# Five statistics of a two-block transformer layer as two rounded products each

## The chip, the cores and the metric

One core of one Trainium2 chip runs the kernel. The metric is the time of one execution on the device in microseconds; a time is the median over runs, and profiles are of one execution. TensorE is called PE, VectorE DVE, ScalarE ACT, GpSimd POOL, SyncE SP.

## The reference

All numbers are float32. Two blocks follow each other on 512 tokens of 1024 features. The first is a mixer (pooling and neighbourhood attention, with 256 context rows) and a squared-ReLU MLP. The second has three mixers side by side (latent attention, a gated recurrence, attention over 256 memory rows) and a gated MLP. Normalizations by the root of the mean square stand everywhere. The change touches five of them:

```python
def rmsnorm(x, g):
    xf = x.astype(jnp.float32)
    y = xf * lax.rsqrt(jnp.mean(xf * xf, axis=-1, keepdims=True) + EPS) * g.astype(jnp.float32)
    return y.astype(x.dtype)

# mla_group: the query latents, 384 features of 512 tokens
q = (rmsnorm(c_q, q_a_norm) @ w_uq).reshape(B, S, MLA_HEADS, QK_HEAD)
# mem_group: the memory's keys, 4 heads of 128 features, 256 rows
k = rmsnorm(k, mem_k_norm)
```

## The kernel before

Features lie on the 128 partitions, tokens along the free axis. The kernel does every large product in three parts: each operand is split into a rounded part (type fp32r, names that end in H, made by ACT) and the rest (names that end in L, made by DVE, for weights by POOL), and PE adds hi times hi, hi times lo and lo times hi into a PSUM bank (`products`, L597 to L599). PE works on rounded operands faster than on full float32 ones.

Weights come in chunks of eight 128x128 blocks (128x1024), in one order planned ahead. SP loads a chunk into one of four `raw` buffers; ACT writes the rounded part to `wH` (L1341, in `ahead`), POOL the rest to `wL` (L2719); three of each are kept. PE waits for the signal of `wL` (L592) before the first product of a chunk. Every engine has one program, written out by hand, and does its instructions in that order; `s.x` are the signals (semaphores) between them, and `Queue.wait_ge` waits for a count.

A statistic is the sum of squares over features, which lie on partitions: PE multiplies a tile of squares by a 128x128 tile of ones in full float32 (`statistic`, L654 to L660, the product is L658) into bank 7, and ACT takes the root from there (`root`, L1357 and L1359) as the exponential of minus half the logarithm.

- **mk0 to mk3**, the memory keys' heads, 256 columns each, stand in the first half of the first MLP's second product, `w_mlp_out`, one behind each of the first four of eight tiles (L941 to L946). A tile has 16 blocks of weights, 48 products, and uses two chunks. ACT squares the keys into `tm[3]` at the start of iteration m (L1605), then splits the tile's weights, takes the root and copies the tile out. DVE multiplies the keys by the root (L2318).
- **lq**, the query latents, 512 columns. It stands in the stage where pieces of dense products (`dense(d)`) are laid between other work; `STEPS` gives the order for all engines. In steps 24 to 42 the other work is memory attention: in item i, PE does the scores (L674), transposes P of item i-2 (L682, `turn`) and weighs the values of item i-3; DVE takes the maximum (L2009), scales it (L2598) and normalizes (P, L2018); ACT does the exponential (L1369). In each step `dense(d)` comes ahead of the item. The latent tiles `c32[0..4]` are made by DVE (`taken`, L2502), squared by ACT (`latent_square`), and POOL adds the squares of the first three into `acc[0]` (L2909, steps 13 and 15). PE does the statistic at step 25. The latents' rounded parts are made by ACT in steps 24, 25 and 27 (`latent_high`, L1352), their rests by DVE from step 25 (`latent_low`, L2508). In step 24 ACT also squares latent tile 3, which DVE makes in the same step.

`root("lq")` is taken by ACT at step 26 and first used by DVE at step 29.

Of the kernel before, what the change touches and what calls it, by code (L numbers as in the profile page):

```python
# [202 lines left out]
class Queue:  # L203
# [20 lines left out]
    "w_hi w_lo product "  # L224

    "summed root "

    "ones sel silu_c mod_mm mod_row mod_col mod_ab coef_a mod_acc mod_sum mod_late coef_b coef_c "


    "sq add_v add_g hi mult full rest_v rest_g lo "

    "x_scaled "

    "u pad q k v_ctx v_a v_v pooled pool_mm pool_y bias "

    "scores biased top expd recip scaled turned turned_sb weighed attended "

    "mix y y_sq m_sq k_mem v_mem post sq_sum "
    "mk_sq mk_n relu relu_sq y_half y_full lb_v lb_a "  # L240

    "y_part post2 add2 x_copied f_raw sig gate kk q_raw q_silu masks angle trig vt_a vt_v "
    "r0_mm r0_cp r0_px r0_v r0_ex r0_a r0_g r1_mm r1_cp r1_px r1_v r1_ex r1_a r1_g "

    "mq mq_sq roots_mm roots_col gg om_n gg_silu gg_n "

    "lat qp qp_sq qp_g kg k_sq kg_g rope_mm rope qn qn_sq kn kn_sq kb k_n col col_sb vl_mm vl_a vl_v "

# [36 lines left out]
def rooted(name):  # L285

    return 2 * ROOTS.index(name) + 2


# [95 lines left out]
def build(nc, xt, xn, ctxt, memt, pos, wall, vec, cst, invc, hmask, rpbw, poolw, out):  # L385
# [5 lines left out]
    K = 1024  # L391
# [23 lines left out]
    small = [at("small", t0 + 6464 + 32 * i, [128, 8]) for i in range(6)]  # L415
    R = t0 + 6656


# [159 lines left out]
    def tensor_program():  # L578
# [75 lines left out]
        def statistic(name, parts, n=512):  # L654
# [5 lines left out]
            freed[7] = s.root, logged(name)  # L660

        def four_sums(b, squares, first, half):

            o = bank[b] if half else claim(b)
            pe.wait_ge(s.sq, first + 4 * half + 4)
            for n in range(4):
                mm = matmul(o[32 * n:32 * n + 32, :], ones[:, 0:32], squares[:, 4 * half + n, :], start=half == 0,
                            stop=half == 1)
            mm.then_inc(s.sq_sum, 1)
# [125 lines left out]
        def value_rows_of_first():  # L795
            order = (4, 5, 0, 1, 2, 3)
            rows("w_in", 12, range(8), tokens(hcH, hcL, XC, 2) + tokens(hH, hL, X1, 4), order, first_scores, s.v_ctx)
            for i in order:
                freed[i] = (s.v_v, {4: 1, 2: 2}[i]) if i in (2, 4) else (s.v_a, {5: 1, 3: 2, 1: 3, 0: 4}[i])
# [125 lines left out]
        for half in range(2):  # L925
            ms = [16 * half + m for m in range(16)]
            if half == 0:
                group([("w_mlp_in", m) for m in ms[:4]], range(8), X2)
                for m in ms[:4]:
                    freed[BANK["w_mlp_in", m]] = s.lo, LO.b + m + 1  # L930
                ms = ms[4:]
            for m in ms:
                tile("w_mlp_in", m, range(8), [(claim(BANK["w_mlp_in", m]), X2)],
                     beside=(lambda k: late_column(5, k)) if m == 4 else None)
                freed[BANK["w_mlp_in", m]] = s.lo, LO.b + m + 1

            def XB(k):
                return bH[:, k % 16, :], bL[:, k % 16, :], s.lo, LO.b + k + 1

            for m in range(8 - half):  # L940
                b = BANK["w_mlp_out", 8 * half + m]  # L941
                tile("w_mlp_out", m, range(16 * half, 16 * half + 16), [(claim(b), XB)])
                freed[b] = (s.y_full if half else s.y_half), m + 1
                if half == 0 and m < 4:
                    pe.wait_ge(s.mk_sq, m + 1)
                    statistic(f"mk{m}", [(tm[3][:, 0:256], 0, 128)], 256)  # L946

# [186 lines left out]
        def value_rows(n):  # L1134

            outs = [claim(BANK["vl", 2 * n + i]) for i in range(2)]
            for k in range(2):
                w_h, w_l, raise_ = weights("w_ukv_2", k, 4, 4)
                x_h, x_l, sem, value = CK(k)
                pe.wait_ge(sem, value)  # L1140
                for i, o in enumerate(outs):
                    t = slice(256 * n + 128 * i, 256 * n + 128 * i + 128)
                    mm = products(o, x_h[:, t], x_l[:, t], w_h, w_l, k == 0, k == 1)
            if n == 0:
                mm.then_inc(s.vl_mm, 1)
            else:
                mm.then_inc(s.product, 1)
            for i in range(2):
                freed[BANK["vl", 2 * n + i]] = (s.vl_a if i else s.vl_v), n + 1
# [7 lines left out]
        def dense(d):  # L1157
            if d < 28:
# [7 lines left out]
                if d == 9:  # L1166
                    pe.wait_ge(s.mq_sq, 4)
                    four_heads("mq", msq)
                if d == 13:
                    turn_roots("mq", 0, mroot)  # L1170
                if d == 25:
                    pe.wait_ge(s.add_g, ADD_G.lat + 2)
                    statistic("lq", [(acc[0][:, :], 0, 128)])
            elif d < 30:
# [149 lines left out]
    def scalar_program():  # L1324
# [36 lines left out]
        def square(dst, src, sem):  # L1361
            activation(dst, src, ACT.Square).then_inc(sem, 1)

        def exponent(a, i):
            g, w = a.base + i, a.w(i)
            act.wait_ge(s.top, a.one + i + 1)
            act.wait_ge(s.roots_col, 1 if a is memory else 2)
            o = bank[a.sc(i)][:, 0:w]
            activation(o, o, ACT.Exp, bias=small[i % 6][:, 0:1], scale=a.scale(i),  # L1369
                       accum_out=small[i % 6][:, 1:2]).then_inc(s.expd, 1)  # L1370
# [115 lines left out]
        act.wait_ge(s.mod_acc, 24)  # L1486
        act.wait_ge(s.v_ctx, 1)
        copy(vC[:, 1, :], bank[5], s.v_a)
# [84 lines left out]
        def hidden(m):  # L1573
# [11 lines left out]
            copy(bH[:, m % 16, :], b, s.hi)  # L1585

        for half in range(2):
            for m in range(16 * half, 16 * half + 16):
# [11 lines left out]
            for m in range(8):  # L1600
                if half == 0 and m < 4:
                    act.wait_ge(s.k_mem, m + 1)
                    if m:
                        act.wait_ge(s.summed, summed(f"mk{m - 1}"))
                    square(tm[3][:, 0:256], kM[:, m, :], s.mk_sq)  # L1605
                for k in range(16 * half, 16 * half + (1 if half and m == 7 else 16)):
# [186 lines left out]
        def dense(d):  # L1793
# [14 lines left out]
            if d % 2 == 0 and 2 <= d <= 8:  # L1808
                m = d // 2 - 1
                act.wait_ge(s.mq, m + 1)  # L1810
                if m in (0, 2):
                    act.wait_ge(s.summed, summed("h3"))
                square(msq[m][:, :], qM[:, m, :], s.mq_sq)
            if d == 10:
# [3 lines left out]
            if d == 28:  # L1818
# [3 lines left out]
                copy(kg[:, :], kg[:, :], s.kg_g, vc("mla_k_r"))  # L1822
            if d == 24:
                for m in range(3):
                    latent_high(m)
# [25 lines left out]
            if d in (39, 42):  # L1851
                if d == 39:
                    act.wait_ge(s.vl_mm, 1)
                    act.wait_ge(s.col_sb, 1)
# [122 lines left out]
    def vector_program():  # L1977
# [25 lines left out]
        def late_vector(sec, at_=0, last=None):  # L2003
            dve.wait_ge(s.mod_sum, (last or sec) - 1)
            tt(mod[:, 8 * sec:8 * sec + 8, 0], STAT[:, at_:at_ + 8], vcs("b_mod")[:, 8 * sec:8 * sec + 8],
               ALU.add).then_inc(s.mod_late, 1)

        def top(a, i):
# [166 lines left out]
        near_top(0)  # L2175
        dve.wait_ge(s.v_ctx, 1)
        dve.wait_ge(s.mod_acc, 24)
# [107 lines left out]
        for half in range(2):  # L2285
# [27 lines left out]
            for m in range(8):  # L2313
                if half == 0:
                    if m < 4:
                        dve.wait_ge(s.root, rooted(f"mk{m}"))
                        dve.wait_ge(s.ones, 5)
# [217 lines left out]
        def dense(d):  # L2535
            if d % 2 == 0 and 2 <= d <= 28:
                taken(d // 2 - 1)
            if d == 14:
                root_columns(0, 128.0 ** -0.5)
            if d == 25:  # L2540
                latent_low(0)
# [39 lines left out]
            if d in (39, 42):  # L2581
                i = 0 if d == 39 else 2
                if d == 39:
                    dve.wait_ge(s.vl_mm, 1)
                    dve.wait_ge(s.col_sb, 1)
# [571 lines left out]
```

## Time and profile before

| | |
|---|---|
| median of 3 runs | 1344.62 us (1344.4 to 1345.4) |
| the profiled execution | 1345.02 us |
| its span, first to last instruction | 1343.7 us |
| PE busy | 1333.6 us, 99% |
| PE weight loads (beside PE) | 1077.4 us, 80% |
| POOL, DVE, ACT busy | 629.3, 572.3, 558.6 us |
| granted clock of TensorE | 1.00 |

Busy times are shares of the span. A timeline row gives the start, the duration, the engine, the line, the operation, out<-in with their forms, and in brackets how long the engine was idle before it and who ended that. A full float32 product shows as two records, which stand in one row as x2. Ends of PE's records are modelled, and records of neighbours overlap, so the pace of PE is read from starts.

### The profile page before, as it was taken

The page shows a single profiled execution, that of the slowest core. Times are in us where ns is not written, and L with a number is a line of the kernel's source. Part 1 is how long each engine was busy: PE and PEld are TensorE (multiplying, and loading weights), DVE is VectorE, ACT ScalarE, POOL GpSimd, SP SyncE. Part 2 cuts the span into 40 slices and gives each one's busy share as a digit, 9 for nine tenths or more (in the row PEclk, how much of TensorE's full clock was granted, in tenths as well). Part 3 has the DMA queues.
Part 4 walks back from the last instruction along what each step waited for, and adds up shares of the span by engine and source line. Part 5 has one row for each costly group of instructions (what it writes and reads, how often), then busy time and mean ns, then how long its engine had stood idle before and what let it go on. Part 6 is the DMA issues. An engine that isn't in the chain of part 4 may idle for free.

```text
span 1343.7 us, 16536 instructions
## 1 busy us (share of the span) xinstructions
PE 1333.6 (99%) x6610; PEld 1077.4 (80%) x6610; DVE 572.3 (43%) x921; ACT 558.6 (42%) x933; POOL 629.3 (47%) x333
## 2 busy tenths in 40 slices
PE   9999999999999999999999999999999999999999
PEld 6788778888888888888788887776878888888887
DVE  5796786653200152103477657665532221122211
ACT  4522675554432244224565548544542231222220
POOL 3544326944444444555476553642444444344442
DMA  9675235432323333233342112111233233322331
GB/s 380 240 285 200 89 144 188 151 106 83 94 94 101 102 101 97 94 98 117 103 122 63 48 63 66 61 47 48 64 94 94 94 96 108 94 94 94 94 110 62
DMA packets 41228, 150.70 MB, mean 112 GB/s; under 512 B 4288, under 2 KB 4544, under 8 KB 40384
## 3 DMA queue, kind: packets, MB, share of 16 engines
q1 hardware_dynamic: 40272, 146.36, 32.9%
q0 software_dynamic: 448, 2.62, 0.5%
q8 instruction: 52, 0.85, 0.3%
q10 hardware_dynamic: 432, 0.67, 0.1%
q14 instruction: 24, 0.20, 0.0%
HBM read 146.75 MB, written 2.10 MB: 111 GB/s over the span
## 4 chain that ended last, share of the span: by engine, by line
PE 92%; DVE 4%; ACT 2%; DMA 1%; issue 1%; POOL 1%; SPq 0%; DVEq 0%; ACTq 0%; POOLq 0%
PE bank L597 26%; PE bank L599 25%; PE bank L598 25%; PE bank L674 2%; PE bank L1033 2%; PE bank L644 1%; PE bank L645 1%; PE bank L646 1%; PE bank L689 1%; PE bank L658 1%; PE bank L841 1%; PE bank L682 1%; PE bank L822 1%; DVE small L2158 1%; DMA xq<-in_xt 1%
## 5 line engine op out<-in xcount | busy, mean ns | idle before, releaser
L2719 POOL TENSOR_TENSOR wL<-raw,wH 128x1024 fp32r<-128x1024 f32 (+1 forms) x209 | 509.7, 2441 | 573.1 <-ACT wH L1341 570.0
L597 PE MATMUL bank<-hH,wH 128*128 128x512 f32 x784 | 317.0, 404 | 1.3 <-POOL wL L2719 0.6
L599 PE MATMUL bank<-hH,wL 128*128 128x512 f32 x784 | 305.8, 390 | 0.0
L598 PE MATMUL bank<-hL,wH 128*128 128x512 f32 x784 | 305.7, 390 | 0.0
L1341 ACT ACTIVATE wH<-raw 128x1024 fp32r<-128x1024 f32 (+1 forms) x209 | 219.4, 1051 | 191.0 <-PE bank L599 164.0
L597 PEld LDWEIGHTS bank<-hH,wH 128*128 128x128 f32 x784 | 147.4, 188 | 38.2 <-issue 7.1
L599 PEld LDWEIGHTS bank<-hH,wL 128*128 128x128 f32 x784 | 147.2, 188 | 31.8
L598 PEld LDWEIGHTS bank<-hL,wH 128*128 128x128 f32 x784 | 147.5, 188 | 28.8 <-issue 1.9
L597 PE MATMUL bank<-gH,wH 128*128 128x512 f32 x352 | 137.6, 391 | 0.0
L599 PE MATMUL bank<-gH,wL 128*128 128x512 f32 x352 | 137.0, 389 | 0.0
L598 PE MATMUL bank<-gL,wH 128*128 128x512 f32 x352 | 136.9, 389 | 0.0
L597 PE MATMUL bank<-bH,wH 128*128 128x512 f32 (+1 forms) x272 | 103.4, 380 | 0.0
L599 PE MATMUL bank<-bH,wL 128*128 128x512 f32 (+1 forms) x272 | 102.5, 377 | 0.0
L598 PE MATMUL bank<-bL,wH 128*128 128x512 f32 (+1 forms) x272 | 102.4, 376 | 0.0
L597 PEld LDWEIGHTS bank<-gH,wH 128*128 128x128 f32 x352 | 66.1, 188 | 15.6 <-issue 1.9
L2289 DVE SCALAR_TENSOR_TENSOR bank<-bank,tmp 128x512 f32<-128x512 f32 x32 | 22.3, 698 | 131.7 <-ACT tmp L1581 131.7
L598 PEld LDWEIGHTS bank<-gL,wH 128*128 128x128 f32 x352 | 66.1, 188 | 14.0 <-issue 0.2
L599 PEld LDWEIGHTS bank<-gH,wL 128*128 128x128 f32 x352 | 66.1, 188 | 13.7
L598 PEld LDWEIGHTS bank<-bL,wH 128*128 128x128 f32 x272 | 51.2, 188 | 9.5
L599 PEld LDWEIGHTS bank<-bH,wL 128*128 128x128 f32 x272 | 51.2, 188 | 9.5
L597 PEld LDWEIGHTS bank<-bH,wH 128*128 128x128 f32 x272 | 51.2, 188 | 9.3
L2000 DVE SCALAR_TENSOR_TENSOR macc<-rows,vecs,macc 128x1024 f32<-128x1024 f32 x28 | 55.0, 1964 | 2.1 <-DMA rows<-in_wall 0.5
(388 smaller groups left out, 1904.4 us busy)
## 6 DMA issues: line engine op xcount, KB each, us to landing
raw<-in_wall SPq DMA_DIRECT2D x209, 512.0 KB, 3.6
rows<-in_wall SPq DMA_DIRECT2D x24, 1024.0 KB, 11.3
bra<-in_rpbw SPq DMA_DIRECT2D x8, 360.0 KB, 4.3
xq<-in_xt SPq DMA_DIRECT2D x2, 1024.0 KB, 7.1
xT<-in_xn SPq DMA_DIRECT2D x1, 2048.0 KB, 7.9
out_x<-xT SPq DMA_DIRECT2D x8, 256.0 KB, 2.5
vE<-in_ctxt SPq DMA_DIRECT2D x1, 1024.0 KB, 20.6
icn<-in_invc POOLq DMA_DIRECT2D x1, 1024.0 KB, 8.6
```

The costliest lines, as they stand in the source:

```text
L597: matmul(o, a_h, b_h, start=first, stop=False)
L598: matmul(o, a_h, b_l, start=False, stop=False)
L599: return matmul(o, a_l, b_h, start=False, stop=last)
L644: matmul(o, x_h, w_h, start=n == 0, stop=False)
L645: matmul(o, x_h, w_l, start=False, stop=False)
L646: mm = matmul(o, x_l, w_h, start=False, stop=n == len(ks) - 1)
L674: mm = matmul(o[:, c0:c1], lhsT, rhs, start=first, stop=last)
L1033: mm = matmul(o[:, 64 * c:64 * c + 64], e_[:, 128 * c:128 * c + 128], view(e_[:, :], 128 * c + m, [[2 * m, 64 // m], [1, m]]), start=True, ...
L1341: activation(wH[i % NHL][:, 0:n], raw[i % NRAW][:, 0:n], ACT.Copy).then_inc(s.w_hi, 1)
L2000: stt(out=sums, in0=w, scalar=ck, in1=sums, op0=ALU.mult, op1=ALU.add).then_inc(s.mod_acc, 1)
L2289: stt(out=b, in0=b, scalar=0.0, in1=tm[m % 3][:, :], op0=ALU.max, op1=ALU.mult).then_inc(s.relu_sq, 1)
L2719: tt(wL[i % NHL][:, 0:n], raw[i % NRAW][:, 0:n], wH[i % NHL][:, 0:n].bitcast(F32), ALU.subtract).then_inc(s.w_lo, 1)
```

## The change

The five statistics mk0 to mk3 and lq are computed from a rounded part of the squares (`sumH`, written by ACT) and the rest (`sumL`, written by DVE in the place of the squares), as two products with ones of the rounded type. The rounded ones are a copy of `ones`, made once by ACT ahead of the first MLP, in a place where constants of the neighbourhood attention lay. PE waits for both halves. For mk0 to mk3, ACT makes the copy behind the square and DVE the rest ahead of its wait for the root. For lq, both are made in step 24: by ACT behind the square of latent tile 3 and ahead of `latent_high`, by DVE behind `taken`.

Signals are merged: `mk_sq` and `mq_sq` become `head_sq`, `v_ctx` and `vl_mm` become `rows_mm`, with the counts shifted.

```diff
+HALVED = "mk0 mk1 mk2 mk3 lq".split()
+
+def halved(name):
+    return HALVED.index(name) + 1
...
+    ones_r = at("ones", t0 + 4 * O_NA, [128, 128], F32R)
+
+    def halves_of(name):
+        if name[:2] == "mk":
+            return tm[3][:, 0:256], at("sumH", 88 * K, [128, 512], F32R)[:, 0:256], at("sumL", 94 * K, [128, 512], F32R)[:, 0:256]
+        return acc[0][:, :], at("sumH", R + 28 * K, [128, 512], F32R)[:, :], at("sumL", 100 * K, [128, 512], F32R)[:, :]
...
+        def statistic_of_halves(name, n=512):
+            o = claim(7)
+            _, high, low = HALVES[name]
+            pe.wait_ge(s.sums_hi, halved(name) + 1)
+            pe.wait_ge(s.sums_lo, halved(name))
+            matmul(o[:, 0:n], ones_r[:, :], high, start=True, stop=False)
+            matmul(o[:, 0:n], ones_r[:, :], low, start=False, stop=True).then_inc(s.summed, 1)
+            freed[7] = s.root, logged(name)
...
@@ PE, w_mlp_out
                 if half == 0 and m < 4:
-                    pe.wait_ge(s.mk_sq, m + 1)
-                    statistic(f"mk{m}", [(tm[3][:, 0:256], 0, 128)], 256)
+                    statistic_of_halves(f"mk{m}", 256)
...
@@ PE, dense(d)
                 if d == 9:
-                    pe.wait_ge(s.mq_sq, 4)
+                    pe.wait_ge(s.head_sq, 8)
                     four_heads("mq", msq)
...
                 if d == 25:
-                    pe.wait_ge(s.add_g, ADD_G.lat + 2)
-                    statistic("lq", [(acc[0][:, :], 0, 128)])
+                    statistic_of_halves("lq")
...
@@ ACT
+        def high_sums(name, sem, value):
+            act.wait_ge(sem, value)
+            copy(HALVES[name][1], HALVES[name][0], s.sums_hi)
...
+        act.wait_ge(s.bias, 24)
+        copy(ones_r[:, :], ones[:, :], s.sums_hi)
         for half in range(2):
             for m in range(16 * half, 16 * half + 16):
                 ahead("w_mlp_in", 7, max(m, 4))
...
-                    square(tm[3][:, 0:256], kM[:, m, :], s.mk_sq)
+                    square(tm[3][:, 0:256], kM[:, m, :], s.head_sq)
+                    high_sums(f"mk{m}", s.head_sq, m + 1)
...
             if d == 24:
+                high_sums("lq", s.add_g, ADD_G.lat + 2)
                 for m in range(3):
                     latent_high(m)
...
@@ DVE
+        def low_sums(name):
+            dve.wait_ge(s.sums_hi, halved(name) + 1)
+            rest(HALVES[name][2], HALVES[name][0], HALVES[name][1], s.sums_lo)
...
                     if m < 4:
+                        low_sums(f"mk{m}")
                         dve.wait_ge(s.root, rooted(f"mk{m}"))
...
+            if d == 24:
+                low_sums("lq")
             if d == 25:
                 latent_low(0)
```

## Rows read from the trace of the kernel before

**Rows 1.** The page: busy time of PE (us, share of the span, instructions).
```profile
PE 1333.6 (99%) x6610; PEld 1077.4 (80%) x6610; DVE 572.3 (43%) x921; ACT 558.6 (42%) x933; POOL 629.3 (47%) x333
```

**Rows 2.** Busy us by stretch: PE, PEld, DVE, ACT, POOL; then granted clock.
```profile
275.00:640.00 365.00, 364.52 (x1661) 303.45 (x1660) 89.78 (x144) 135.21 (x197) 170.99 (x75) 1.00 0.32 99
...
812.00:882.00 70.00, 70.00 (x371) 54.08 (x369) 45.06 (x106) 46.65 (x95) 37.47 (x24) 1.00 0.19 61
```

**Rows 3.** Timeline of PE at mk0: start us, us, instruction.
```profile
374.13 0.59 PE L658 MATMUL bank<-tmp,ones 128*128 128x256 f32 x2
...
374.79 0.39 PE L598 MATMUL bank<-bL,wH 128*128 128x512 f32 x1
```

**Rows 4.** Timeline of PE, rounded 128x512 products, first and last of 28.
```profile
544.66 0.39 PE L597 MATMUL bank<-bH,wH 128*128 128x512 f32 x1
...
550.78 0.39 PE L597 MATMUL bank<-bH,wH 128*128 128x512 f32 x1
```

**Rows 5.** Timeline of PE, rounded 128x256 products; their weight loads (ns min/median/max).
```profile
246.90 0.28 PE L597 MATMUL bank<-hmH,wH 128*128 128x256 f32 x1
...
247.97 0.28 PE L597 MATMUL bank<-hmH,wH 128*128 128x256 f32 x1
...
L597 PEld LDWEIGHTS bank<-hmH,wH x32: 188/192/192, 246.7 to 258.9; 128*128 128x128 f32 x32
```

**Rows 6.** Timelines of ACT and POOL at mk0 and behind mk1's square.
```profile
365.31 0.41 ACT L1362 ACTIVATE tmp<-kvM 128x256 f32<-128x256 f32 x1
...
376.37 1.05 ACT L1341 ACTIVATE wH<-raw 128x1024 fp32r<-128x1024 f32 x1
...
377.50 2.40 POOL L2719 TENSOR_TENSOR wL<-raw,wH 128x1024 fp32r<-128x1024 f32 x1 [5.02 <-ACT wH L1341]
```

**Rows 7.** Timelines of ACT, POOL and weight loads at 286 to 291 us.
```profile
286.81 2.00 ACT L1341 ACTIVATE wH<-raw 128x1024 fp32r<-128x1024 f32 x2
...
287.94 4.75 POOL L2719 TENSOR_TENSOR wL<-raw,wH 128x1024 fp32r<-128x1024 f32 x2 [6.31 <-ACT wH L1341]
...
290.14 0.19 PEld L599 LDWEIGHTS bank<-hH,wL 128*128 128x128 f32 x1
290.45 0.19 PEld L597 LDWEIGHTS bank<-hH,wH 128*128 128x128 f32 x1
```

**Rows 8.** A group by form (busy us, mean ns); a line's (ns min/median/max).
```profile
L1350 ACT ACTIVATE PTs<-bank 128x128 f32<-128x128 f32 x4 | 1.1, 277 | 8.6 <-PE bank L682 8.6
...
L1983 DVE TENSOR_TENSOR hL<-tmp,hH x3: 691/692/693, 29.2 to 48.8; 128x512 fp32r<-128x512 f32 x3
```

**Rows 9.** Timeline of PE at the latent statistic.
```profile
816.44 1.02 PE L658 MATMUL bank<-acc,ones 128*128 128x512 f32 x2
817.30 0.59 PE L674 MATMUL bank<-kvM,qM 128*128 128x256 f32 x2
```

**Rows 10.** Timelines of ACT and DVE at the latent statistic.
```profile
816.00 0.63 ACT L1362 ACTIVATE acc<-c 128x512 f32<-128x512 f32 x1 [0.47 <-DVE c L2502]
816.54 1.93 ACT L1352 ACTIVATE cH<-c,vecs 128x512 fp32r<-128x512 f32 x3
...
832.21 1.14 ACT L1350 ACTIVATE hH<-gg 128x512 fp32r<-128x512 f32 x2
...
815.88 0.41 DVE L2009 TENSOR_REDUCE small<-bank 128x1 f32<-128x256 f32 x1
```

**Rows 11.** Latent lows on DVE (timeline, then ns min/median/max), and POOL beside them.
```profile
817.28 1.26 DVE L2508 SCALAR_TENSOR_TENSOR cL<-c,vecs,cH 128x512 fp32r<-128x512 f32 x1 [0.73 <-ACT cH L1352]
...
L2508 DVE SCALAR_TENSOR_TENSOR cL<-c,vecs,cH x5: 737/742/2317, 817.3 to 826.7; 128x512 fp32r<-128x512 f32 x5
...
815.61 2.38 POOL L2719 TENSOR_TENSOR wL<-raw,wH 128x1024 fp32r<-128x1024 f32 x1 [7.65 <-ACT wH L1341]
```

**Rows 12.** Timelines at memory item 0: DVE's P, PE's turn.
```profile
819.31 0.48 DVE L2018 TENSOR_SCALAR P<-bank,small 128x256 f32<-128x256 f32 x1
...
820.93 0.38 PE L682 MATMUL bank<-cst,P 128*128 128x128 f32 x2
```

More of the change, by code:

```diff
@@ L228 @@
     "ones sel silu_c mod_mm mod_row mod_col mod_ab coef_a mod_acc mod_sum mod_late coef_b coef_c "
-    "sq add_v add_g hi mult full rest_v rest_g lo "
+    "sq head_sq sums_hi sums_lo add_v add_g hi mult full rest_v rest_g lo "
     "x_scaled "
-    "u pad q k v_ctx v_a v_v pooled pool_mm pool_y bias "
+    "u pad q k rows_mm v_a v_v pooled pool_mm pool_y bias "
     "scores biased top expd recip scaled turned turned_sb weighed attended "
     "mix y y_sq m_sq k_mem v_mem post sq_sum "
-    "mk_sq mk_n relu relu_sq y_half y_full lb_v lb_a "
+    "mk_n relu relu_sq y_half y_full lb_v lb_a "
     "y_part post2 add2 x_copied f_raw sig gate kk q_raw q_silu masks angle trig vt_a vt_v "
     "r0_mm r0_cp r0_px r0_v r0_ex r0_a r0_g r1_mm r1_cp r1_px r1_v r1_ex r1_a r1_g "
-    "mq mq_sq roots_mm roots_col gg om_n gg_silu gg_n "
-    "lat qp qp_sq qp_g kg k_sq kg_g rope_mm rope qn qn_sq kn kn_sq kb k_n col col_sb vl_mm vl_a vl_v "
+    "mq roots_mm roots_col gg om_n gg_silu gg_n "
+    "lat qp qp_sq qp_g kg k_sq kg_g rope_mm rope qn qn_sq kn kn_sq kb k_n col col_sb vl_a vl_v "
     "mix2_hi mix2 part x2_s x2 x2_copy ga silu_g gm gu x_out"
@@ L416, in build @@
     R = t0 + 6656
+    ones_r = at("ones", t0 + 4 * O_NA, [128, 128], F32R)
[3 more added lines that the diff above has]
+        return acc[0][:, :], at("sumH", R + 28 * K, [128, 512], F32R)[:, :], at("sumL", 100 * K, [128, 512], F32R)[:, :]
+    HALVES = {name: halves_of(name) for name in HALVED}
     macc = [at("macc", R + (88 + 4 * i) * K, [128, 1024]) for i in range(2)]
@@ L796, in value_rows_of_first @@
             order = (4, 5, 0, 1, 2, 3)
-            rows("w_in", 12, range(8), tokens(hcH, hcL, XC, 2) + tokens(hH, hL, X1, 4), order, first_scores, s.v_ctx)
+            rows("w_in", 12, range(8), tokens(hcH, hcL, XC, 2) + tokens(hH, hL, X1, 4), order, first_scores, s.rows_mm)
             for i in order:
@@ L1144, in value_rows @@
             if n == 0:
-                mm.then_inc(s.vl_mm, 1)
+                mm.then_inc(s.rows_mm, 1)
             else:
@@ L1486, in scalar_program @@
         act.wait_ge(s.mod_acc, 24)
-        act.wait_ge(s.v_ctx, 1)
+        act.wait_ge(s.rows_mm, 1)
         copy(vC[:, 1, :], bank[5], s.v_a)
@@ L1812, in dense @@
                     act.wait_ge(s.summed, summed("h3"))
-                square(msq[m][:, :], qM[:, m, :], s.mq_sq)
+                square(msq[m][:, :], qM[:, m, :], s.head_sq)
             if d == 10:
@@ L1852, in dense @@
                 if d == 39:
-                    act.wait_ge(s.vl_mm, 1)
+                    act.wait_ge(s.rows_mm, 2)
                     act.wait_ge(s.col_sb, 1)
@@ L2175, in vector_program @@
         near_top(0)
-        dve.wait_ge(s.v_ctx, 1)
+        dve.wait_ge(s.rows_mm, 1)
         dve.wait_ge(s.mod_acc, 24)
@@ L2583, in dense @@
                 if d == 39:
-                    dve.wait_ge(s.vl_mm, 1)
+                    dve.wait_ge(s.rows_mm, 2)
                     dve.wait_ge(s.col_sb, 1)
```

## The prediction

> **What bounds the kernel now.** I read the page's table of engines first, then the busy time by stretch, then the timelines of PE around the five statistics, and last those of ACT, DVE and POOL at the same places. PE is busy for 1333.6 us, 99% of the span [rows 1], and in the two stretches that hold the five statistics (275 to 640 us and 812 to 882 us) it is busy for 364.52 of 365 and 70.00 of 70 us, at a granted clock of 1.00 [rows 2]. So inside these stretches whatever shortens PE's own stream shortens the kernel, whatever makes PE wait lengthens it, and work that is added to ACT, DVE or POOL costs nothing until PE has to wait for it. The same view says how large the stake can be: five statistics of under 1 us each, in 1344.
>
> The sum is made against the profiled execution, 1345.02 us (the span of 1343.7 and 1.3 around it). The median of the runs shown is 1344.62, 0.40 lower; I take that off at the end.
>
> **Part 1: the products of the four key statistics (mk0 to mk3).** Removed, four times: one full-precision 128x256 product, shown as two records. From its start at 374.13 to the second ordinary product behind it at 374.79 are 0.66 us [rows 3]. An ordinary 128x512 product of rounded operands takes 0.227 (27 of them between 544.66 and 550.78) [rows 4], so the statistic holds PE for 0.66 - 0.227 = 0.43 us. Added: two products of rounded operands of 128x256. Nine such run between 246.90 and 247.97, 0.119 us each [rows 5], two are 0.24. Saved: 0.19 us each, 0.77 us for four. A handover between kinds of product could shift this by some hundredths each; I bound the four together at 0.6 to 0.9.
>
> **Part 2: the extra work behind the key statistics.** ACT gets a copy of 128x256 behind each square, and DVE a subtraction. The mk0 square starts at 365.31 and the statistic runs on PE at 374.13 [rows 3, 6]. The copy starts after the square has ended (365.72) and takes about as long as the square, 0.41; the subtraction takes no longer than one of 128x512, 0.69 [rows 8]. The halves are there by 366.9, 7.2 us before PE asks, and mk1 to mk3 have one whole tile of PE (48 products of 0.227, 10.9 us) in the same way. What the copy pushes back is the split of the next weight chunk: behind mk1's square ACT does it at 376.37 (1.05 long) and POOL the low part at 377.50 (2.40 long) [rows 6], ready at 379.9 and now some 0.45 later. Three split chunks are kept and one lasts 24 x 0.227 = 5.4 us, so this one is asked for two chunks after the statistic at 374.1, at about 385.5: 5.6 us of cover for 0.45 us of delay. Cost: nothing; if that cover were gone, 0.45 us each, 1.8 in all.
>
> **Part 3: rounding the ones, once.** ACT copies 128x128 ahead of the split of the chunk at 286.81, which it starts as soon as it is through with the last normed row. Here there is no cover. That split is followed by POOL's low part, which starts at 287.94 and needs 2.4 us, so it ends at about 290.34 [rows 7]; PE's weight load for the first product of this chunk starts at 290.45, 0.31 behind the one before it instead of the usual 0.23 [rows 7]: the chunk is already the last thing that PE waits for, by some hundredths. The trace has no such copy from SBUF; the nearest row is the ACT copy of 128x128 out of PSUM, 277 ns [rows 8], of which some 0.07 would overlap with the next instruction, as each square overlaps with the instruction behind it (816.00 + 0.63 is after 816.54 [rows 10]). I take 0.20 us on the path, with 0 and 0.35 as ends. The wait for the bias signals in front of it is long over at 286 us. The second chunk in this pair is ready at 292.7 and asked for at 296, so nothing follows.
>
> **Part 4: the latent statistic's product.** One full-precision 128x512 product: from 816.44 to the next instruction's start at 817.30, 0.86 us [rows 9]. Two rounded ones: 2 x 0.227 = 0.45 us [rows 4]. Saved: 0.40 us.
>
> **Part 5: the latent statistic's operands.** This is where the change loses. Its sum of squares has been lying in acc for long; before, PE ran the statistic at 816.44 without a wait. Now the two halves are made in step 24 of the interleaved stage, just ahead of PE's need in step 25, and each engine's queue decides when. On ACT the new copy stands behind the square of the fourth latent tile, which waits for DVE's product of this tile and starts at 816.00; the instruction behind that square starts at 816.54 [rows 10]. The copy takes that place. A copy of 128x512 between SBUF tiles into a rounded one lasts about 0.6 (two in 1.14) [rows 10], so the high half is there at 817.14. DVE, with the semaphore, can start at 817.17. Its subtraction takes 0.69 on 128x512 from SBUF [rows 8]: 817.86.
>
> But POOL runs a low part of weights from 815.61 to 817.99 [rows 11], and the DVE rows show what that does to an operation with two inputs in SBUF: the first latent low at 817.28 takes 1.26 us where 0.74 is the median, so it really worked from 817.28 + 1.26 - 0.74 = 817.80, 0.2 before POOL's end; the longest of the five takes 2.32 [rows 11]. Our subtraction also reads two SBUF tiles, so I let it work from 817.80: finished at 818.49, PE goes on at 818.53 with a hop of some hundredths. PE's wait: 818.53 - 816.44 = 2.09 us. Without the hold it would be 817.90 - 816.44 = 1.46. Upper end: held as long as the longest row, 2.32, from 817.17: 819.5, a wait of 3.1.
>
> The Trainium skill states this against the change (SBUF — State Buffer, section "Who interferes with whom"): a VectorE instruction with two SBUF inputs contends with a GpSimd instruction that reads SBUF, and the one that comes second waits for the whole of the other. With the rule the sum is the one below, without it 0.63 us less; the trace agrees with it by the 1.26 and 2.32 us above.
>
> What is queued behind the new waits: on ACT the three high latent halves, later by 0.54, and the exponent of memory item 0; on DVE the maximum of item 0, which ran at 815.88 [rows 10] and now runs at about 818.4. The chain of item 0 ended with P at 819.31 + 0.48 = 819.79, and PE asked for it at 820.93 [rows 12]: 1.1 us of room. DVE's new order is maximum 818.4, scaled maximum 818.9, two latent lows to 820.4, P to 821.0, while PE asks at 820.93 + 1.7 = 822.6 with all of PE's shift. No new wait; the shift of PE covers the delay of DVE (1.2 us). Nothing near absorbs the shift: PE has no idle time from 812 to 882 us [rows 2], and all that follows on the other engines is released by PE.
>
> **Part 6: the rest.** Merging four signals into two moves no instruction; the waits for the merged counts come at the places of the old ones. Nothing is added to a DMA queue, none is passed.
>
> **Sum:** -0.77 (1) + 0 (2) + 0.20 (3) - 0.40 (4) + 2.09 (5) = +1.12 us. Profiled execution 1345.02 + 1.12 = 1346.1; median 1344.62 + 1.12 = 1345.7 us. With the ends of every part: -0.9 + 0 - 0.4 + 1.46 = +0.2 to -0.6 + 0.35 - 0.4 + 3.1 = +2.5, so 1344.8 to 1347.1.
>
> **Rivals.**
> (a) The halves of lq are not late: PE's shift is absorbed, or ACT and DVE reach them before PE does. For it: the sum of squares is complete long before, and only the place in two queues delays it. Against it: the square at 816.00 and the copy's place at 816.54 are after PE's own 816.44. Then -0.77 - 0.40 + 0.20 = -0.97: 1343.6 us. 13%.
> (b) The cascade, slower: DVE is held once more in the memory items, because its two-input operations now stand elsewhere against POOL's 2.4 us ones, and P comes later than PE's turn. It decides at memory item 0 or 1 [rows 12]: if DVE falls behind PE by more than the 1.1 us of room, PE waits again, once or twice, up to one POOL operation (2.40) each. Price 1.12 + 1 to 2.4: 1346.7 to 1348.1 us. For it: DVE is busy for 45.06 of 70 us there [rows 2], and each item's operations stand in one queue with the latent lows. Against it: PE itself has been moved back by the same stall. 15%.
> (c) It does not do what it says on PE: two products of 256 columns cost as much as the full-precision one, because the weights are loaded twice and a load lasts 188 ns, longer than 119. Against it: the products at that pace load new weights each time, with loads as long [rows 5]. Then part 1 is 0: +1.9, 1346.5. 4%.
>
> **How the numbers follow.** My forecast has 68%. Range: from (a), 1343.6 less a little for the spread of a median (the three runs lie 1344.4 to 1345.4), to the lower half of (b): 1343.5 to 1347.3. A measurement of this kernel tells about 0.2% from no change, 2.7 us: faster means under 1341.9, slower over 1347.3. Nothing in the sum reaches 1341.9 (all gains without any cost are 1.3 us): 3% for what I have not seen. Slower: half of (b) and a little of the rest, 10%. Same: 87%.
>
> **What would show it.** Each key statistic as two products about 0.12 us apart, without a wait before it, and the interval between statistics shorter by 0.19. A copy of 128x128 on ACT at about 286.8 and a gap of 0.2 on PE at 290.6. At about 815.6 (the place of 816.44, less what has been saved before) a gap of 2 us on PE that ends with DVE's subtraction, which shows over 1 us of duration. No gap over 0.3 us at the turns of the memory items. I am wrong if there is no such gap, if a gap of its size appears at a later item, or if the time is outside 1344.8 to 1347.1.

## The result, and the profile after

The changed kernel takes 1347.18 us (median of 22 runs, 1345.59 to 1348.28), the kernel before 1344.86 (22 runs, 1344.23 to 1345.64). The ratio is 1.0016, with a 95% interval of 1.001 to 1.0021 (it is not the quotient of the medians, and can differ from it a little): slower by some 2.2 us. The median was forecast at 1345.7, with 1343.5 to 1347.3 as the range.

The median hides two groups. Ten of the 22 runs have a mean granted clock of 1.000 and lie at 1345.59 to 1346.69; twelve have 0.999 and lie at 1347.03 to 1348.28. Together with 11 more runs of the same kernel (e1_after) there are 13 at 1.000, median 1345.8, and 20 at 0.999, median 1347.6. The kernel before has its clock on record in the runs beside the experiments: 1.000 in each of the 80 that are compared; one more, 1899.15 us at a clock of 0.655, fell in a slow state of the chip and is left out of every number here. The profiled execution, 1345.59 us with a span of 1344.3, is of the first group.

Busy time by stretch, columns as in [rows 2]:

```profile
275.00:640.00 365.00, 364.18 (x1661) 302.89 (x1660) 92.20 (x150) 137.79 (x202) 171.08 (x76) 1.00 0.33 99
...
812.00:882.00 70.00, 67.93 (x361) 52.93 (x363) 45.92 (x107) 45.76 (x94) 37.47 (x24) 1.00 0.20 61
```

The stretch from 275 us is as full as it was: the 0.34 us that are missing against [rows 2] are one wait for a tile of DVE (`hL`), which stands at 639.53 here and stood at 640.87 before, outside the stretch. In the second, PE is busy for 67.93 of 70 us, where it was 70.00 [rows 2]: 2.07 us are missing, in one place.

The timeline of PE at mk0:

```profile
373.65 0.28 PE L687 MATMUL bank<-sumH,ones 128*128 128x256 f32 x1
373.76 0.28 PE L688 MATMUL bank<-sumL,ones 128*128 128x256 f32 x1
373.88 0.40 PE L617 MATMUL bank<-bH,wH 128*128 128x512 f32 x1
```

The two rounded products of 256 columns hold PE from 373.65 to 373.88, 0.23 us, where the full-precision one held it for 0.43 [rows 3]. That statistic starts 0.48 us earlier than before (373.65 against 374.13). The execution was already 0.65 us ahead when the change began (ACT's split behind the last normed row would stand at 286.16 against 286.81 [rows 7]), so 0.17 were lost in between. PE's timeline shows where:

```profile
289.74 0.39 PE L619 MATMUL bank<-hH,wL 128*128 128x512 f32 x1
290.04 0.47 PE L617 MATMUL bank<-hH,wH 128*128 128x512 f32 x1
290.34 0.40 PE L618 MATMUL bank<-hL,wH 128*128 128x512 f32 x1
```

From 289.74 to 290.34 are 0.60 us for two products, where two take 0.45 [rows 4]: the first product of the chunk whose split stands behind the copy of the ones.

PE at the latent statistic, then ACT, DVE and POOL there:

```profile
814.89 0.39 PE L619 MATMUL bank<-hH,wL 128*128 128x512 f32 x1
817.34 0.47 PE L687 MATMUL bank<-sumH,ones 128*128 128x512 f32 x1 [2.07 <-DVE sumL L2019]
817.65 0.40 PE L688 MATMUL bank<-sumL,ones 128*128 128x512 f32 x1
817.89 0.59 PE L703 MATMUL bank<-kvM,qM 128*128 128x256 f32 x2
```

```profile
814.67 0.63 ACT L1389 ACTIVATE acc<-c 128x512 f32<-128x512 f32 x1 [0.47 <-DVE c L2543]
815.21 0.61 ACT L1377 ACTIVATE sumH<-acc 128x512 fp32r<-128x512 f32 x1
```

```profile
815.86 1.34 DVE L2019 TENSOR_TENSOR sumL<-acc,sumH 128x512 fp32r<-128x512 f32 x1 [1.22 <-ACT sumH L1377]
817.12 0.41 DVE L2049 TENSOR_REDUCE small<-bank 128x1 f32<-128x256 f32 x1
```

```profile
814.28 2.37 POOL L2762 TENSOR_TENSOR wL<-raw,wH 128x1024 fp32r<-128x1024 f32 x1 [7.65 <-ACT wH L1368]
```

PE waits 2.07 us for sumL, where [rows 9] show the statistic without a wait. ACT makes the high half at 815.21, behind the square of tile 3. DVE starts its subtraction at 815.86; it takes 1.34 us, not 0.69 [rows 8], and ends at 817.20. POOL's low part of weights ends at 814.28 + 2.37 = 816.65, and 817.20 less 0.69 is 816.51, the same 0.1 to 0.2 us before POOL's end as in [rows 11].

P of memory item 0 and PE's request for item 2 and the turn behind it:

```profile
819.21 0.48 DVE L2058 TENSOR_SCALAR P<-bank,small 128x256 f32<-128x256 f32 x1
```

```profile
821.06 0.59 PE L703 MATMUL bank<-kvM,qM 128*128 128x256 f32 x2
```

P ends at 819.69 and PE comes at 821.06: no new wait, as before [rows 12].

### The profile page after: what moved, and what is told of

Same layout as the page of the kernel before. It is cut to its first block, busy times and chain, and to the rows that moved or that the text cites. A ratio compares the mean times of both kernels' runs of the same rounds, so it can differ in the third digit from the quotient of the medians.

```text
span 1344.3 us, 16546 instructions
## 1 busy us (share of the span) xinstructions
PE 1333.3 (99%) x6610; PEld 1078.2 (80%) x6610; DVE 574.9 (43%) x926; ACT 561.3 (42%) x939; POOL 626.9 (47%) x333
## 4 chain that ended last, share of the span: by engine, by line
PE 93%; DVE 4%; ACT 2%; issue 1%; POOL 1%; DVEq 0%; POOLq 0%; ACTq 0%
PE bank L617 26%; PE bank L619 25%; PE bank L618 25%; PE bank L703 2%; PE bank L1061 2%; PE bank L664 1%; PE bank L665 1%; PE bank L666 1%; PE bank L718 1%; PE bank L870 1%; PE bank L851 1%; PE bank L711 1%; PE bank L678 1%; PE bank L759 1%; DVE small L2198 1%
```

## The experiments

Two theories stood after the result. **A:** PE's wait at the latent statistic costs about 1 us net in every execution, and in some it also lowers the clock, for some 2 us more. **B:** the second group has another cause (the chip, the loads, the keys' products). Runs are compared with the kernel before on the same chip; a kernel has 11 runs, e7_long_gap has 4. Three chips took part, and the medians of the kernel before there are 1344.86 (e1 to e4), 1344.96 (e5 to e8) and 1344.92 us (e9 and e10).

**e1_after.** The changed kernel itself, once more.

> The changed kernel again, to see whether its spread is its own (22 executions lay between 1345.59 and 1348.28 us, 12 of them with a mean granted clock of 0.999 and all of them above 1347.0, while 22 of the kernel before lay within 1.4 us). Theory A (the wait sets off the clock): PE's wait of 2.1 us at the latent statistic costs 1.0 us net in every execution and in about half of them also lowers the granted clock for a short stretch, another 1 to 2 us: again two groups, near 1345.9 and 1347.6. Theory B (the spread has nothing to do with the wait, but comes with the chip or the loads of the day): the kernel before shows the same two groups on this chip.

Measured: 1347.27 us, ratio 1.0017 (1.0008 to 1.0025). Three runs at clock 1.000 (1345.41 to 1346.26), eight at 0.999 (1347.10 to 1348.06). The kernel before, beside it: 1344.86 us (32 runs, 1344.11 to 1345.34), no such group. The two groups belong to the changed kernel.

**e2_early.** The latent halves are made before PE needs them.

```diff
@@ ACT
-            if d == 24:
+            if d == 18:
                 high_sums("lq", s.add_g, ADD_G.lat + 2)
+            if d == 24:
                 for m in range(3):
@@ DVE
-            if d == 24:
+            if d == 20:
                 low_sums("lq")
```

> Both halves of the latent statistic are made earlier, the high one by ACT in step 18, the low one by DVE in step 20; all else as changed. Theory A: PE's wait at the latent statistic goes (2.1 us) and with it the group at clock 0.999; what is left is -0.84 for the keys' products, -0.3 to -0.4 for the latent one, +0.17 for the rounded ones: 1.0 us under the kernel before, near 1343.9, in one group. Theory B: the two groups stay. Rival C (the extra ACT and DVE work itself is what costs, wherever it stands, since the recurrence in steps 18 to 23 has no room either): the time stays at or above the kernel before, 1345 or more, with new waits of PE on the recurrence's operations.

Measured: 1343.74 us, 1.12 under the kernel before by the medians, ratio 0.9994 (0.9985 to 1.0003), all eleven runs at clock 1.000. The interval still holds no change at all. The latent subtraction, by its tile (ns min/median/max, first start):

```profile
L2020 DVE TENSOR_TENSOR sumL<-acc,sumH x1: 681/681/681, 792.1 to 792.1; 128x512 fp32r<-128x512 f32 x1
```

It stands at 792.1 us, 23 us ahead of PE's use, and takes 0.68. The recurrence found room for both operations, so rival C of the expectation falls. The latent part brings less than its products say, though. The starts of the scores of memory items 0 and 1 are 3.66 us apart, where they were 4.06: the 0.40 are won. But from item 3 to item 4 they are 4.28 apart, where they were 4.03, most of it ahead of the transpose behind the scores, which comes 0.61 us after them instead of 0.43. From the first item's scores to the last's the whole is 54.30 us for the 54.43 of the kernel before, so 0.13 us are left of the 0.40.

**e3_keys_only.** The latent statistic as before the change.

```diff
                 if d == 25:
-                    statistic_of_halves("lq")
+                    pe.wait_ge(s.add_g, ADD_G.lat + 2)
+                    statistic("lq", [(acc[0][:, :], 0, 128)])
...
-                high_sums("lq", s.add_g, ADD_G.lat + 2)
...
-            if d == 24:
-                low_sums("lq")
```

> Only the four keys' statistics as two rounded products; the latent one is a full-precision product of the summed squares as before, with nothing made in step 24. Theory A: -0.84 + 0.17 = -0.67 us, near 1344.2, one group at clock 1.000. Theory B: two groups here too. If the keys' part loses, it is above the kernel before.

Measured: 1344.25 us, 0.61 under the kernel before by the medians, ratio 0.9995 (0.9986 to 1.0004), all at 1.000. The median lies where the keys' products put it, though the interval also holds no change; the keys' part does not touch the clock.

**e4_filler.** PE works while it waits. The nine products are extra work whose results are overwritten.

```diff
                 if d == 25:
+                    claim(7)
+                    for _ in range(9):
+                        matmul(bank[7], ones_r[:, :], hH[:, 0, :], start=True, stop=True)
                     statistic_of_halves("lq")
```

> As changed, and PE fills its wait at the latent statistic with nine rounded 128x512 products (9 x 0.227 = 2.0 us) into the bank that the statistic then overwrites; they change no result. Theory A: PE is never idle there, so the clock does not fall: one group at clock 1.000 near 1345.9, what the unlucky executions lose is gone while the 2.1 us stay. Theory B: still two groups, to 1348.

Measured: 1345.99 us, ratio 1.0009 (1.000 to 1.0018), all eleven at 1.000 (1345.45 to 1346.50). PE's timeline:

```profile
815.08 2.20 PE L1202 MATMUL bank<-hH,ones 128*128 128x512 f32 x9
817.34 0.47 PE L687 MATMUL bank<-sumH,ones 128*128 128x512 f32 x1
```

The statistic starts at 817.34, to the hundredth where it starts in the changed kernel. So the halves are as late as they were, and only PE's idleness has gone; the second group went with it. This separates the two prices: 1.13 us (1345.99 less 1344.86) for the late halves with all that the products gain, and 1.28 more by the median (1347.27) for a PE that is idle meanwhile, 1.5 more in the executions of the second group (1347.45 is their median beside this kernel).

**e5_high_first.** Is it ACT's queue that makes the subtraction late, or POOL?

```diff
@@ ACT, dense(d)
+            if d == 24:
+                high_sums("lq", s.add_g, ADD_G.lat + 2)
             if d in (10, 12, 14, 24, 26):
                 latent_square((10, 12, 14, 24, 26).index(d))
...
             if d == 24:
-                high_sums("lq", s.add_g, ADD_G.lat + 2)
                 for m in range(3):
```

> ACT makes the latent statistic's high half ahead of the square of latent tile 3 instead of behind it; all else as changed. ACT is free from about 814.2 us, so the high half is there by about 814.8 and DVE can start its subtraction right behind its product (about 814.8 instead of 815.86). Theory H (the subtraction is held by POOL's low part of weights, 814.28 to 816.65): it still ends at about 817.1 with a duration of over 2 us, PE waits 2.0 us as before, and the time stays at two groups, 1345.6 and 1347.5. Rival Q (only the place in ACT's queue counts): it takes 0.69, is done by 815.5, PE waits 0.4 us, and the time is near 1344.2 in one group.

Measured: 1346.56 us, ratio 1.0013 (1.0004 to 1.0021), six runs at 1.000 (1345.23 to 1346.56), five at 0.999 (1347.09 to 1347.81). DVE's subtraction and POOL's operation:

```profile
815.55 2.45 DVE L2020 TENSOR_TENSOR sumL<-acc,sumH 128x512 fp32r<-128x512 f32 x1
```

```profile
815.08 2.37 POOL L2763 TENSOR_TENSOR wL<-raw,wH 128x1024 fp32r<-128x1024 f32 x1 [7.66 <-ACT wH L1368]
```

The subtraction lasts 2.45 us and ends at 818.00; less 0.69 that is 817.31, 0.14 before POOL's end (817.45). PE waits 2.07 us, as in the changed kernel. It started 0.47 us behind POOL's operation instead of 1.58, and it ended with it all the same. An earlier high half gains nothing while POOL's operation runs. The Trainium skill has this as a lock (SBUF — State Buffer, section "Who interferes with whom"), and the runs agree: with POOL's operation in the way the same subtraction takes 1.34 and 2.45 us, without it 0.68 and 0.69.

**e6_gap_only.** The wait alone, with the full-precision product. The halves are made and not used.

```diff
-        return acc[0][:, :], at("sumH", ...)[:, :], at("sumL", 100 * K, [128, 512], F32R)[:, :]
+        return acc[0][:, :], at("sumH", ...)[:, :], at("sumL", R + 26 * K, [128, 512], F32R)[:, :]
...
-                    statistic_of_halves("lq")
+                    pe.wait_ge(s.sums_hi, halved("lq") + 1)
+                    pe.wait_ge(s.sums_lo, halved("lq"))
+                    statistic("lq", [(acc[0][:, :], 0, 128)])
```

> PE waits for both halves of the latent sums as changed, but then does the full-precision product of the sums as the kernel before (the halves are made and not used; the low one goes to a buffer of its own). Theory A: the wait alone does it: 0.4 us over the changed kernel, and again two groups, near 1346.2 at clock 1.000 and 1348 at 0.999. If the second group comes from the rounded products behind the wait instead, it is gone: one group near 1346.2.

Measured: 1347.09 us, ratio 1.0016 (1.0007 to 1.0025). Five runs at 1.000, median 1346.2, six at 0.999, median 1347.9: both groups where theory A has them. The profiled execution (1348.34 us) is one of the second group, and so the one in which the clock can be seen. Stretches of 1 us; the column behind POOL's is the granted clock:

```profile
816.00:817.00 1.00, 0.07 (x1) 0.00 (x0) 0.34 (x1) 1.00 (x3) 1.00 (x1) 1.00 0.00 0
817.00:818.00 1.00, 0.00 (x0) 0.00 (x0) 1.00 (x2) 1.00 (x3) 0.46 (x1) 1.00 0.00 0
818.00:819.00 1.00, 0.89 (x2) 0.49 (x3) 0.96 (x4) 0.84 (x2) 0.00 (x0) 1.00 0.56 70
819.00:820.00 1.00, 1.00 (x5) 0.75 (x4) 0.98 (x3) 0.89 (x3) 0.00 (x0) 0.69 0.75 274
820.00:821.00 1.00, 1.00 (x4) 0.81 (x3) 0.95 (x3) 0.00 (x0) 0.00 (x0) 0.50 0.50 197
821.00:822.00 1.00, 1.00 (x4) 0.81 (x3) 1.00 (x3) 0.88 (x3) 0.00 (x0) 0.50 0.00 0
822.00:823.00 1.00, 1.00 (x4) 0.77 (x4) 0.90 (x3) 1.00 (x2) 0.20 (x1) 0.60 0.00 0
823.00:824.00 1.00, 1.00 (x6) 0.83 (x5) 0.00 (x0) 0.97 (x3) 1.00 (x1) 1.00 0.00 0
```

PE has been idle since 816.07 and starts again at 818.1. The granted clock is still 1.00 in the stretches of the wait; from 819 on it is 0.69, 0.50, 0.50 and 0.60, then 1.00 again. 0.50 is the lower level, 1.2 GHz. What is missing from 1.00 in these four stretches is 1.71 us together, and 1.71 in a span of 1347.0 is a mean of 0.999, the mark of the second group. PE itself slows down with it:

```profile
818.11 1.10 PE L678 MATMUL bank<-acc,ones 128*128 128x512 f32 x2 [2.03 <-issue]
819.04 0.71 PE L703 MATMUL bank<-kvM,qM 128*128 128x256 f32 x2
...
820.83 0.63 PE L617 MATMUL bank<-hH,wH 128*128 128x512 f32 x1
821.26 0.63 PE L618 MATMUL bank<-hL,wH 128*128 128x512 f32 x1
...
823.36 0.39 PE L618 MATMUL bank<-hL,wH 128*128 128x512 f32 x1
823.59 0.39 PE L619 MATMUL bank<-hH,wL 128*128 128x512 f32 x1
823.81 0.59 PE L703 MATMUL bank<-kvM,qM 128*128 128x256 f32 x2
```

From 820.83 to 821.26 is one rounded product, 0.43 us, against 0.23 from 823.36 to 823.59. From the scores of item 1 at 819.04 to those of item 2 at 823.81 are 4.77 us; in the changed kernel, at full clock, 817.89 to 821.06 are 3.17. The clock has cost 1.60 us here.

**e7_long_gap.** A longer wait. ACT repeats its copy five times, and the counts that DVE and PE wait for are raised so that both go on only behind the last.

```diff
                 high_sums("lq", s.add_g, ADD_G.lat + 2)
+                for n in range(5):
+                    act.wait_ge(s.sums_hi, 6 + n)
+                    copy(HALVES["lq"][1], HALVES["lq"][0], s.sums_hi)
...
@@ PE, statistic_of_halves
-            pe.wait_ge(s.sums_hi, halved(name) + 1)
+            pe.wait_ge(s.sums_hi, halved(name) + (6 if name == "lq" else 1))
...
@@ DVE, low_sums
-            dve.wait_ge(s.sums_hi, halved(name) + 1)
+            dve.wait_ge(s.sums_hi, halved(name) + (6 if name == "lq" else 1))
```

> ACT copies the high half five times more before DVE may go on, so that PE waits about 3 us longer at the latent statistic (4.6 to 5.2 us in all). Theory A: the granted clock falls in every execution or nearly so, the profile shows a stretch at the lower level behind the wait, and the time is about 1345.6 + 3 + 2 = 1350.5, in one group. Rival (the clock falls by chance, whatever the wait): a group at clock 1.000 near 1348.7 stays.

Measured: 1350.11 us, ratio 1.0041 (1.0027 to 1.0054), all four runs below 1.000 (three at 0.999, one at 0.997). The end of the wait on PE, and the granted clock by stretch:

```profile
820.06 0.47 PE L687 MATMUL bank<-sumH,ones 128*128 128x512 f32 x1 [4.73 <-DVE sumL L2022]
```

```profile
819.00:820.00 1.00, 0.00 (x0) 0.00 (x0) 0.78 (x2) 1.00 (x3) 0.00 (x0) 1.00 0.59 242
820.00:821.00 1.00, 0.94 (x3) 0.84 (x4) 0.96 (x3) 1.00 (x3) 0.00 (x0) 0.70 0.00 0
...
822.00:823.00 1.00, 1.00 (x4) 0.77 (x3) 0.96 (x4) 0.18 (x1) 0.00 (x0) 0.50 0.00 0
...
824.00:825.00 1.00, 1.00 (x6) 0.83 (x5) 0.81 (x3) 1.00 (x2) 0.29 (x1) 1.00 0.00 0
```

4.73 us of wait, and the clock falls in the stretch in which PE starts again. No run stayed at 1.000, but four runs are few: if the shorter wait's share of 31 in 55 held here too (the sum of e1, e5, e6 and the result), four in a row would come by chance about one time in ten.

**e8_ones_covered.** e2_early, with the ones rounded later.

```diff
-        act.wait_ge(s.bias, 24)
-        copy(ones_r[:, :], ones[:, :], s.sums_hi)
         for half in range(2):
             for m in range(16 * half, 16 * half + 16):
                 ahead("w_mlp_in", 7, max(m, 4))
+                if m == 4:
+                    act.wait_ge(s.bias, 24)
+                    copy(ones_r[:, :], ones[:, :], s.sums_hi)
```

> As e2_early, and the ones are rounded four tiles later, behind the split of weights for tile 4 of the first MLP. The loss of 0.1 to 0.2 us at 290 us should go: near 1343.6, 1.3 us under the kernel before, one group. If the copy now delays the relu of tile 4 for PE, it is 1343.8 or more.

Measured: 1343.79 us, 1.17 under the kernel before by the medians, ratio 0.9993 (0.9984 to 1.0002), all at 1.000. The place on PE:

```profile
289.75 0.39 PE L619 MATMUL bank<-hH,wL 128*128 128x512 f32 x1
289.98 0.40 PE L617 MATMUL bank<-hH,wH 128*128 128x512 f32 x1
290.21 0.40 PE L618 MATMUL bank<-hL,wH 128*128 128x512 f32 x1
```

0.46 us for the two products that took 0.60 in the changed kernel: the loss there is gone, 0.14 us. In the time it can't be seen beside e2_early (1.12 under its own kernel before, against 1.17).

**e9_pool_behind.** POOL lets DVE go first.

```diff
@@ POOL, dense(d)
+            if d == 24:
+                pool.wait_ge(s.sums_lo, 5)
             if d < 28:
                 ahead("w_in_2", 4 * (d % 2) + 3, BESIDE[d // 2])
```

> As changed, but POOL does its low part of weights of step 24 only after DVE's subtraction for the latent statistic. Theory H (POOL's operation holds the subtraction): it now takes 0.69 instead of 1.34 us, PE waits about 1.45 instead of 2.07 us, and the group at clock 1.000 lies 0.6 us lower, near 1345.1; whether a wait of 1.45 us still lowers the clock in some executions is open, the fewer the better for theory A. Rival: the 1.34 us come from something else, the duration and the wait stay, and PE may wait again for the weights that POOL makes later.

Measured: 1346.36 us, ratio 1.0013 (1.0004 to 1.0021), all eleven at 1.000. DVE's subtraction and the two latent lows, POOL's operation, and PE's waits (us in total, times, longest):

```profile
815.92 0.69 DVE L2019 TENSOR_TENSOR sumL<-acc,sumH 128x512 fp32r<-128x512 f32 x1 [1.22 <-ACT sumH L1377]
...
817.11 3.18 DVE L2549 SCALAR_TENSOR_TENSOR cL<-c,vecs,cH 128x512 fp32r<-128x512 f32 x2
```

```profile
816.69 2.39 POOL L2762 TENSOR_TENSOR wL<-raw,wH 128x1024 fp32r<-128x1024 f32 x1 [10.00 <-DVE sumL L2019]
```

```profile
PE bank L687 <- DVE sumL L2019: 1.4, 1, 1.4
...
PE bank L703 <- DVE P L2058: 0.3, 1, 0.3
```

The subtraction takes 0.69 and PE's wait there falls from 2.07 to 1.42 us, as theory H says. The 0.6 us are not seen in the time, where near 1345.1 was expected: POOL's operation now stands against the two latent lows, which take 3.18 us together instead of 1.41. P of item 0 ends at 820.88, and PE waits 0.30 us for its bank at 820.94. By the starts of the scores, 0.65 us are won from item 0 to item 1 against the changed kernel (5.32 for 5.97), and 0.93 are lost again up to item 4 (0.47, 0.11 and 0.35), so this kernel is 0.28 us longer in this stage than the changed one at full clock. The hold has only changed its victim. Still, no run left clock 1.000.

**e10_later.** PE asks one step later.

```diff
@@ PE
-                if d == 25:
+                if d == 26:
                     statistic_of_halves("lq")
@@ ACT
-            if d == 26:
+            if d == 27:
                 act.wait_ge(r_v[1], 10)
                 root("lq", 384, rs[1])
-            if d == 27:
                 latent_high(4)
```

> As changed, but PE does the latent statistic one step later (26 instead of 25) and ACT takes its root in step 27; the halves are made where the change makes them. PE has some 3 us of other products first. Theory A: no wait of PE there, no group at clock 0.999, about what e2_early gives, near 1343.8. Rival: the root is late for DVE's products with it in step 29 and PE waits there instead: over 1344.5.

Measured: 1345.07 us, ratio 1.0002 (0.9993 to 1.0011), all at 1.000. The expected 1343.8 was missed. PE no longer waits for the halves, but here:

```profile
PE bank L703 <- DVE P L2057: 0.8, 1, 0.8
```

0.84 us at the scores of item 2, for the bank that P of item 0 frees (L2057). From the scores of item 1 to those of item 2 are 4.66 us, where 3.20 and the two products' 0.45 would be 3.65: 1.0 us, most of the 1.3 that the expectation missed. This is the wait of rival (b), and it appears because PE is not held back any more while DVE still is. Late halves cost PE twice: at the statistic, or behind it.

## Why the prediction was right, and where it was short

**Part 1** held: 0.23 us for two products where 0.24 was forecast, mk0 to mk1 0.21 us shorter than before (373.65 to 384.79 against 374.13 to 385.48) where 0.19 was forecast. (The place given for PE's arrival at lq, 815.6, left out part 3's 0.20; by the prediction's own sum it is 815.87. The 0.65 us by which this execution was ahead are most of the difference to 815.12.) From mk0 to PE's arrival at lq (815.12, one product behind 814.89), 0.84 us were gained, where the parts say 0.77.

**Part 2** held: no wait of PE in the stretch that was not there before; e3_keys_only shows the gain alone, 0.61 us by the medians with the ones' cost in it.

**Part 3** held: 0.14 to 0.17 us for 0.20, in the place named; e8_ones_covered takes it away.

**Parts 4 and 5** held, better than they had to: a wait of 2.07 us for 2.09, with DVE's subtraction at 1.34 us. From PE's due start at 815.12 to the next instruction at 817.89 are 2.77 us for the 0.86 of before, so +1.91 where 2.09 - 0.40 = 1.69 was forecast. By starts PE is 2.22 us late (817.34), a little more than the idle time that the row shows, and the first product behind the wait takes 0.31 us to the next start instead of 0.23. The hold, which e5 and e9 confirm, was read off right.

**The sum**, against the checkpoints of the profiled execution: 0.65 ahead at 286 us, 0.17 lost, 0.84 gained, 1.91 lost, 0.6 behind at the end (1344.3 against 1343.7). That is +1.24 for the change, where +1.12 was forecast, and the group at clock 1.000 has its median at 1345.8 for the forecast 1345.7. The nearness of these two times is in part luck: the forecast stood on the median of three runs, 1344.62, and 22 runs give 1344.86; against that the group is 0.95 us up.

**What failed** is the step at the end of part 5 and in the sum, where PE's wait was priced at its own length: "-0.77 (1) + 0 (2) + 0.20 (3) - 0.40 (4) + 2.09 (5) = +1.12". It had no term for the granted clock. [Rows 2] gave 1.00 for this stretch, with PE busy for all of it, and I took the clock for a constant. A PE that idles for 2.07 us found the clock lowered in 20 of 33 executions, for 1.6 us in the one that a trace shows and about 1.8 by the medians of the two groups. So the median moved by 2.3 us and not 1.1, outside the bounds of the parts (1344.8 to 1347.1), which I had named as a sign of being wrong. That it still lies in the range, 0.12 us under the upper end, is luck: that end was drawn for rival (b), which did not happen. Even the median's place is chance in part, because it goes with the larger group, 12 of 22 here; with two executions more in the other group it would have lain there, near 1346.7. The 2.3 us are also less than the 2.7 us that the prediction took as the least that can be told from no change, and yet the interval excludes no change. e4_filler shows the cause by taking it away, e6_gap_only shows the clock itself, and in e7_long_gap, with a longer wait, none of four runs kept it.

**Rival (a)** did not happen, nor (c). **Rival (b)** did not happen in the changed kernel, but its mechanism is real and was named in its right place: e9 and e10 bring it out, with 0.30 and 0.84 us. The room was less than I said: PE first needs P of item 0 for the scores of item 2 (the bank they share), 0.43 us ahead of the turn that I took, so 0.7 and not 1.1 us. With PE held back by 2 us this did not matter. My claim that "the shift of PE covers the delay of DVE" was right, and e10 is its proof: take the shift away and the delay shows.

What stays open: why one execution with the same wait keeps its clock and the next does not. No run tells. The wait's length and the clock beside it are seen together only in profiled executions; that the second group of the changed kernel lost its clock at this very place is taken over from e6_gap_only, since both profiles of the changed kernel fell in the first group. And no run has a wait between 1.42 and 2.03 us.

The version that beats the changed kernel is e2_early or e8_ones_covered, with the halves made six and four steps earlier. By medians it is 1.12 and 1.17 us under the kernel before, and 3.4 to 3.5 under the changed one; the intervals against the kernel before (0.9985 to 1.0003 and 0.9984 to 1.0002) still hold no change. Most of what the traces show as won is the keys' (0.84 us); of the latent part's 0.40 they leave 0.13 to 0.18.

## What to carry to other kernels

Where PE is full, splitting a product in two faster ones pays only if the operands are ready before PE comes; place their making by the queues of the engines that make them, many steps ahead where there is slack, not beside the use. Look for what POOL runs at that moment when DVE gets an operation with two SBUF inputs: here it finished about its own length after POOL's end, less 0.1 to 0.2 us, and pushing POOL back moved the wait to the next such operation. And price an idle time of PE in a full stretch above its length: here 2 us of it cost some 1.6 to 1.8 us more in over half of the executions. If the wait can't go, useless products in it can keep the clock. A median over runs that fall in two groups says little; look at the groups.

## What the runs showed of the hardware that I had not expected

The granted clock of TensorE fell from 2.4 to 1.2 GHz behind a single idle time of PE of 2.03 to 2.07 us (as the profiled executions have it), in 31 of 55 executions of three kernels (20 of 33, 5 of 11, 6 of 11, by their mean clock and time), with PE busy for 99.8% of the time from 300 to 800 us. In both traces that show it (e6_gap_only and e7_long_gap) it fell within about 1.3 us after PE had started again, not during the idle time, and read under 1.00 in four stretches of 1 us. Behind 1.42 us of idle time it fell in none of 11, behind 4.73 us in all 4, and with products in place of the idle time in none of 11. The kernel before has no idle time of PE over 1.34 us, and kept 1.000 in all 80. The profile of one execution does not tell of this: two profiles of the changed kernel showed 1.00 throughout, and only the list of runs, with their clocks of 1.000 and 0.999 and their times in two groups, pointed to it.
